# Hybrid trunk kernel, first part rebuilt: a convolution tile on TensorE, softmax order, shared copies, new weight slots

## Chip, cores and metric

One Trainium2 chip, one core. The metric is the device time of one execution in microseconds (us); of several executions the median is given. All data are 32-bit floats.

## What is computed

Two layers over 256 tokens of width 1024. In each layer a vector `c` gives six modulation vectors (shift, scale, gate for each half). The first half is attention over selected keys beside a convolution module, the second a product-key expert lookup:

```python
mod = (silu(c) @ w_ada[l] + b_ada[l])                 # 1024 x 6144 weights a layer
sh1, sc1, g1, sh2, sc2, g2 = split(mod, 6)
h = rms_norm(x) * (1 + sc1) + sh1
q, k, v, qi, ki, wi, cu = split(h @ w_in[l], offs)
attn = dsa_attention(q, k, v, qi, ki, wi)             # top 64 keys by an index score, 8 heads
a, g = split(cu, 2); u = a * sigmoid(g)
conv = silu(layer_norm(depthwise_conv31(u) + conv_b)) # 512 channels, 31 taps, causal
mixed = concat([rms_norm(attn), rms_norm(conv)])
x = x + g1 * (mixed @ w_out[l])
h2 = rms_norm(x) * (1 + sc2) + sh2
s = (h2 @ w_q) against sub_keys                       # 8 heads, 2 x top 16 of 128, then top 16 of the sums
x = x + g2 * sum_e softmax(top_s) * gelu(u_e . h2) * v_e   # 128 rows of peer_u and of peer_v a token
```

## The kernel before

The 256 tokens are two tiles of 128, and there are two layers, so the work is in four parts, p = 2 * layer + tile. Each part has a first half (`first`, then `attend`) and a second (`second`). For the expert lookup a part gathers 128 rows of `peer_u` and then 128 rows of `peer_v` for every token: 512 indirect DMAs of each in the whole kernel, each of one row of 4 KB for each of 128 partitions, issued by POOL (`u_item`, `v_item`). DVE takes the dot product of each gathered `u` row with h2 (`dots_to`), PE adds up the `v` rows (`v_to`). The rows land in a ring of 13 slots (`rows`); POOL waits for a slot before it issues (`wait_slot_free`), and for the chosen experts: the first 16 rows of part 0 wait for `head_ready`, the next 16 and then each block of 32 for `sel_ready`. DVE raises these after `choose` and `decode` of blocks 0 to 3, and between the blocks of part 0 it has fixed numbers of dot products to do (`FIRST_DOTS`: none, then up to 14, 30 and 46).

All other weights come through SP, in one order that a planner writes out (`plan`, list `seq`). A block of weights has two pieces (512 columns, in descriptors of 2 KB) or four (kinds in `WIDE`: 1024 columns, 4 KB), each piece 1 MB. Until the first part is over there are 13 slots for them: four in `wring`, others in memory that is used otherwise later (slots 4 to 9 are places of `rows`, 10 is `diag_eq`, 11 and 12 are `spread_c`). Later only the four of `wring` are left. SP issues the pieces strictly in the plan's order, and before each it waits until the piece that held the slot has been used (`wait_weight_used`); a piece on a slot that is not free holds back all behind it. `LATE_SLOT` (9) also waits for `conv_full`, because the convolution's sum `acc` lies there. `SLOTS_OF` places the later blocks of the first part by hand.

The modulation vectors of both layers are computed piecewise in between. `("ada", l, j)` is a product by PE (four pieces), `("adaT", l, j)` its turn into columns or its spreading to rows; the dictionary `ADA` says at which place of the program (`"conv"`, `"S"`, `"mix"`, `"out"`, `"wq0"`, ...) each one stands, and plan, PE and ACT follow it alike. Two of them (0, 2) and (0, 4) are computed by DVE (`ada_product`, blocks `adav`).

The jobs of PE pass through a ring of four PSUM banks (0 to 3) in the order of `seq`; ACT or DVE takes each out and frees the bank. PE, ACT and DVE each run their part of the program in a fixed order.

Part 0 in the order of PE: products (0, 0) and (0, 1), turn of h (`turn_h`) and of the modulation, `proj_turned_wide` for the convolution's input, then qi, ki, q, the index scores, k, v, products (1, 0) and (1, 1) (place `"conv"`), turns of q and k, logits, turned probabilities, the turn of the convolution's sums (waits for DVE and POOL), `values`, the turns of the sub-keys, place `"mix"`, the turn of `mixed` (`mT`), the output projection, place `"out"`, the turn of h2, and then the expert queries: `proj_heads` (two jobs of block `wq` 0), `proj_turned` (blocks 1 to 3), with subkeys and the places `"wq0"` to `"wq3"` in between. Then comes `project(1)`, which is the input projection of part 1. The convolution of part 0 runs as 31 multiply-adds for each of four channel tiles of 128: tiles 0 to 2 on DVE (`taps`, in four portions between other work, `TAP_STEPS`), tile 3 on POOL. In parts 1 to 3 it runs on PE with diagonal matrices made by ACT (L902). DVE's `glu(1)` is between its blocks 2 and 3 and waits for `ca` and `cg` of `project(1)`.

Of the kernel before, what the change touches and what calls it, by code (L numbers as in the profile page):

```python
# [16 lines left out]
P = 128  # L17
# [48 lines left out]
TAP_STEPS = (24, 18, 25)  # L66
# [6 lines left out]
def turn(l, j):  # L73
# [59 lines left out]
def plan():  # L133
# [30 lines left out]
    for p in range(PARTS):  # L164
# [15 lines left out]
        if p == 0:  # L180
# [9 lines left out]
            for name in ("k", "v"):  # L190
                both(name, p)
# [21 lines left out]
        if p == 0:  # L213
            for i in range(2):
                job("lnB", l, i)
            ada(p, "S")
# [4 lines left out]
        if p == 0:  # L221
            both("sk", p)
            ada(p, "mix")
# [4 lines left out]
        else:  # L228
# [3 lines left out]
            ada(p, "out")  # L232
        for q in range(2):
            job("h2T", p, q)
# [26 lines left out]
def trunk(nc, x, c, positions, w_ada, b_ada, w_in, q_norm_g, k_norm_g, idx_k_ln_g, idx_k_ln_b,  # L261
# [53 lines left out]
    with ExitStack() as ctx:  # L315
# [127 lines left out]
        conv_dve = sem("conv_dve")  # L443
        conv_pool = sem("conv_pool")
# [70 lines left out]
        def wait_weight_used(eng, i):  # L515

            name = uses[i][0]
            if uses[i] in vec_count:
# [37 lines left out]
        def tap_diag(p, n, j):  # L556

            return diags[:, n % 2, j, :]

# [27 lines left out]
        def _(sp):  # L587
            sp.dma_start(ccol[:, :], c[0, :].rearrange("(p k) -> p k", k=KT)).then_inc(c_landed, 16)

            def source(name, h):  # L590
# [9 lines left out]
                if kind in WIDE:  # L600
                    a = 1024 * name[2] if a is None else a
                    return w[:, 2 * h:2 * h + 2, a:a + 1024]
                a = 512 * name[2] if a is None else a
# [3 lines left out]
            for i, (name, h) in enumerate(uses):  # L607
# [25 lines left out]
                else:  # L633
                    w = weight_slot(slot).rearrange("p (k n) -> p k n", k=2 if name[0] in WIDE else 4)
# [68 lines left out]
        def _(pe):  # L703
# [120 lines left out]
            def proj_heads(block, rhs, between):  # L824

                w = [piece(block, 0), piece(block, 1)]
                for c, name in enumerate(jobs_of(block)):
                    if c:
                        between()
                    b, o = open_job(*name)  # L830
                    for i in range(2):
                        for k in range(KT):
                            at = (2 * c + i) * P
                            ins = pe.matmul(o[:, i * P:(i + 1) * P], w[k // 4][:, k % 4, at:at + P], rhs[:, k, :],
# [167 lines left out]

            def first(p):
# [25 lines left out]
                def subkey_turns():  # L1029
# [942 lines left out]
```

## Time and profile before

| | us |
|---|---|
| median of 3 runs | 1902.33 |
| lowest and highest | 1896.08, 1903.36 |
| span of the profiled execution | 1733.4 |
| own time of the profiled execution, with what lies around the span | 1902.3 (the median; 168.9 around the span) |
| bytes moved | 691.98 MB, mean 399 GB/s |

The profile is of one execution. Its span is from the first to the last instruction; what lies around it is taken as the difference of span and median, since the profiled execution has no other time. The 16 DMA engines are busy almost throughout: 9 tenths or more in nearly every slice of the page. PE is busy for 60% of the span, DVE 64%, POOL 59%, ACT 16%.

### The profile page before, as it was taken

What the parts mean: (1) busy time and instruction counts of PE and PEld (TensorE: products, weight loads), DVE (VectorE), ACT (ScalarE), POOL (GpSimd) and SP (SyncE); (2) the same over time, 40 slices, a digit from 0 to 9 for tenths busy, and PEclk for the clock granted to TensorE, in tenths of its full rate; (3) what the DMA queues carried; (4) which work ended last, traced back from release to release, by engine and by line L of the source; (5) the groups of instructions that cost most, each with busy time, mean ns of one, the idle gap of its engine ahead of it and who ended that gap; (6) DMA issues with size and microseconds to landing.
All of it is one profiled execution on the core that took longest, in us unless ns stands there. A gap on an engine that the chain in (4) does not pass through costs nothing.

```text
span 1733.4 us, 18207 instructions
## 1 busy us (share of the span) xinstructions
PE 1039.2 (60%) x6158; PEld 590.6 (34%) x6158; DVE 1103.2 (64%) x3003; ACT 273.4 (16%) x717; POOL 1015.9 (59%) x1133
## 2 busy tenths in 40 slices
PE   7979897406896588603788569611689610005555
PEld 4547674303363156301345146500236200001111
DVE  1987989996218576888117676889513979991000
ACT  2141235202110035300101024400210100000000
POOL 2610435676655763566755664567655777776774
PEclk8989899657998799655899679765899865557888
DMA  9998999999999999999999999999999999999998
GB/s 373 393 368 327 405 405 383 409 409 409 409 409 407 408 404 410 397 410 397 410 409 409 394 409 408 399 407 409 406 406 402 391 410 410 409 410 389 409 409 330
DMA packets 195481, 691.98 MB, mean 399 GB/s; under 512 B 21360, under 2 KB 21376, under 8 KB 195134
## 3 DMA queue, kind: packets, MB, share of 16 engines
q0 software_dynamic: 147840, 537.06, 78.1%
q1 hardware_dynamic: 47550, 153.77, 22.8%
q8 instruction: 49, 0.80, 0.2%
q14 instruction: 42, 0.34, 0.1%
HBM read 689.71 MB, written 1.05 MB: 398 GB/s over the span
## 4 chain that ended last, share of the span: by engine, by line
DMA 41%; PE 24%; DVE 15%; POOL 13%; issue 6%; ACT 1%; SPq 0%; DVEq 0%; ACTq 0%; POOLq 0%
DMA rows<-in_peer_v,v_at 20%; DMA rows<-in_peer_u,u_at 18%; PE ps L921 8%; DVE rows L1586 8%; PE ps L876 7%; POOL rows L698 7%; POOL rows L690 6%; DMA kiw<-in_w_in 1%; PE ps L818 1%; PE ps L864 1%; PE ps L848 1%; DMA rows<-in_w_ada 1%; DVE rows L1568 1%; PE ps L735 1%; PE ps L804 1%
## 5 line engine op out<-in xcount | busy, mean ns | idle before, releaser
L690 POOL DMA_INDIRECT rows<-in_peer_u,u_at x512 | 482.5, 942 | 370.8 <-DVE dots L1586 202.5
L1586 DVE CUSTOM_DVE_ANT_0 rows<-rows,ps 128x1024 f32<-128x1024 f32 x512 | 610.3, 1219 | 92.5 <-DMA rows<-in_peer_u,u_at 78.6
L698 POOL DMA_INDIRECT rows<-in_peer_v,v_at x512 | 485.7, 949 | 283.9 <-PE ps L921 153.4
L921 PE MATMUL ps<-rows,spread_c 128*32 128x512 f32 x2048 | 325.7, 764 | 215.0 <-DMA rows<-in_peer_v,v_at 215.0
L735 PE MATMUL ps<-ident 128*128 128x128 f32 x228 | 39.9, 346 | 354.3 <-DVE dots L1586 354.3
L921 PEld LDWEIGHTS ps<-rows,spread_c 128*32 128x32 f32 x2048 | 71.4, 125 | 414.8 <-issue 412.6
L735 PEld LDWEIGHTS ps<-ident 128*128 128x128 f32 x228 | 35.6, 183 | 369.8 <-DVE dots L1586 356.6
L876 PEld LDWEIGHTS ps<-hT,wring 128*128 128x128 f32 x1152 | 137.0, 199 | 25.7 <-issue 24.1
L876 PE MATMUL ps<-hT,wring 128*128 128x128 f32 x1152 | 142.2, 285 | 0.0
L848 PE MATMUL ps<-wring,hT 128*128 128x512 f32 x256 | 117.1, 600 | 8.3 <-DMA wring<-in_w_in 7.5
L902 PE MATMUL ps<-diag_eq,hc 128*128 128x128 f32 x744 | 104.7, 307 | 25.3 <-ACT diag_eq L1274 25.2
L1274 ACT ACTIVATE diag_eq<-ident,cwT 128x128 f32<-128x128 f32 x372 | 111.6, 387 | 30.4 <-PE ps L902 29.1
L902 PEld LDWEIGHTS ps<-diag_eq,hc 128*128 128x128 f32 x744 | 100.7, 220 | 31.6 <-ACT diag_eq L1274 29.8
L1599 DVE TENSOR_TENSOR gy<-ps,g 128x512 f32<-128x512 f32 x8 | 5.5, 689 | 162.3 <-PE ps L921 162.2
L1796 DVE MAX8 v<-mixed_use 128x8 f32<-128x128 f32 x64 | 15.7, 286 | 122.0 <-ACTq L1234 120.1
L1231 ACT COPY mixed_use<-ps 128x512 f32<-128x512 f32 (+1 forms) x54 | 30.7, 569 | 294.1 <-PE ps L876 157.9
L848 PEld LDWEIGHTS ps<-wring,hT 128*128 128x128 f32 x256 | 46.1, 190 | 69.5 <-issue 53.5
L1495 ACT ACTIVATE dots<-dots 128x128 f32<-128x128 f32 x4 | 1.2, 309 | 381.8 <-DVE dots L1586 381.8
L1895 DVE TENSOR_TENSOR gy<-ps,g 128x512 f32<-128x512 f32 x8 | 5.5, 692 | 73.1 <-PE ps L848 70.4
L1586 DVE DVE_READ_ACCUMULATOR2_ANT dots<- 128x1 f32 x512 | 42.1, 82 | 0.0
L1242 ACT ACTIVATE hT<-ps,modcol 128x128 f32<-128x128 f32 x52 | 19.5, 456 | 135.0 <-PE ps L729 134.3
L788 PE MATMUL ps<-wring,cact 128*32 128x512 f32 x192 | 27.1, 683 | 7.0 <-DMA wring<-in_w_ada 7.0
(254 smaller groups left out, 1183.9 us busy)
## 6 DMA issues: line engine op xcount, KB each, us to landing
wring<-in_w_in SPq DMA_DIRECT2D x34, 1024.0 KB, 13.2
wring<-in_w_ada SPq DMA_DIRECT2D x31, 1024.0 KB, 10.6
wring<-in_peer_wq SPq DMA_DIRECT2D x28, 1024.0 KB, 9.6
rows<-in_w_ada SPq DMA_DIRECT2D x16, 1024.0 KB, 14.9
wring<-in_w_out SPq DMA_DIRECT2D x13, 1024.0 KB, 17.1
rows<-in_peer_u,u_at POOLq DMA_INDIRECT x512, 14.1
rows<-in_peer_v,v_at POOLq DMA_INDIRECT x512, 9.5
rows<-in_w_in SPq DMA_DIRECT2D x6, 1024.0 KB, 15.9
```

Source lines behind the costliest of these rows:

```text
L690: pool.indirect_dma_start(row(n), None, u_rows, bass.IndirectOffsetOnAxis(ap=u_at[:, p % 2, k:k + 1], axis=0)).then_inc(row_landed[n % SLO ...
L698: pool.indirect_dma_start(row(n), None, v_rows, bass.IndirectOffsetOnAxis(ap=v_at[:, p % 2, tok:tok + 1], axis=0)).then_inc(row_landed[n % ...
L735: pe.transpose(ps[:, spare, 0:P], ident[:, :], ident[:, :])
L788: ins = pe.matmul(o[32 * g:32 * g + 32, :], cact[:, k:k + 1].to_broadcast([P, 32]), ws[:, i, 512 * cc:512 * cc + 512], start=h == 0, stop= ...
L848: ins = pe.matmul(o, lhs[:, k, :], w[:, j, 512 * cc:512 * cc + 512], start=k == 0, stop=k == KT - 1)
L876: ins = pe.matmul(o[:, i * P:(i + 1) * P], w[:, j, at:at + P], rhs[:, k, :], start=False, stop=(k, i) == (KT - 1, 3))
L902: ins = pe.matmul(o[:, cols], hc[:, ct, t * P + i:t * P + i + P], tap_diag(p, n, i - i0), start=False, stop=i == TAPS - 1)
L921: ins = pe.matmul(ps[32 * g:32 * g + 32, YB + q, :], spread_c[:, g, a, :], row(n)[:, q * 512:q * 512 + 512], start=a == 0, stop=a == 31)
L1231: act.copy(dst, o if src is None else src(o)).then_inc(free[b], 1)
L1242: ins = act.activation(hT[:, k, :], o[:, i * P:(i + 1) * P], ACT.Identity, bias=0.0 if shift is None else shift[:, k:k + 1], scale=scale[: ...
L1274: ins = act.activation(tap_diag(p, n, i - i0), ident[:, :], ACT.Copy, scale=cwT[:, ct, i:i + 1])
L1586: dve.tensor_tensor_reduce(out=row(n), in0=row(n), in1=h2_shown, scale=1.0, scalar=0.0, op0=ALU.mult, op1=ALU.add, accum_out=dots[:, k:k + ...
```

## The change

In part 0:

- Channel tile 0 of the convolution moves from DVE to PE (`conv_first`, 31 matmuls and one for the bias, after k). ACT makes its 31 diagonal matrices ahead in `g1`, `g2` and `skT` (`first_diag`). DVE has 62 steps in place of 93, all before the logits.
- v's projection and `lnB` change places on PE: `lnB` after k, v after the logits. The convolution's sums are turned right after v, ahead of the softmax's turned probabilities, without the 20 spare transposes; three tiles are turned, not four. ACT loads its exponential's table ahead.
- Of h's eight copies from PSUM ACT makes four and DVE four; the turn of (0, 0) comes ahead of the product (0, 1).
- The places of the modulation blocks are new: product (0, 3) and turn (0, 2) at `"conv"`, turn (0, 3) at `"S"`, product (1, 0) at `"mix"`, product (1, 1) at `"wq0"`, turn (1, 0) and product (1, 3) at `"wq1"`, turn (1, 1) and product (1, 4) at the new `"wq2"`. The sub-keys are loaded and turned after the output projection.
- `SLOTS_OF` is new. Block `wq` 0 is loaded as two pieces by head, 256 columns each (descriptors of 1 KB), so its first piece is free after the first head's job.

```diff
-TAP_STEPS = (24, 18, 25)
+TAP_STEPS = (24, 18, 20)
...
-    (0, "pre2"): [product(0, 1)],
-    (0, "preT"): [turn(0, 0), turn(0, 1)],
-    (0, "conv"): [product(1, 0), product(1, 1)],
-    (0, "S"): [turn(1, 0), turn(1, 1)],
-    (0, "mix"): [turn(0, 2), product(0, 3)],
-    (0, "out"): [turn(0, 3), turn(0, 4)],
-    (0, "wq0"): [product(1, 3)],
-    (0, "wq1"): [product(1, 4)],
+    (0, "pre2"): [turn(0, 0), product(0, 1)],
+    (0, "preT"): [turn(0, 1)],
+    (0, "conv"): [product(0, 3), turn(0, 2)],
+    (0, "S"): [turn(0, 3)],
+    (0, "mix"): [product(1, 0)],
+    (0, "out"): [turn(0, 4)],
+    (0, "wq0"): [product(1, 1)],
+    (0, "wq1"): [turn(1, 0), product(1, 3)],
+    (0, "wq2"): [turn(1, 1), product(1, 4)],
...
-SLOTS_OF = {("sk", 0): (2,), ("ada", 0, 3): (3, 4, 5, 6), ("out", 0, 0): (7, 8), ("adav", 0, 4): (0, 1, LATE_SLOT, 2),
-            ("out", 0, 1): (DIAG_SLOT, 3), ("wq", 0, 0): (5, 6), ("ada", 1, 3): (4, 7, 0, 8), ("wq", 0, 1): (1, LATE_SLOT),
-            ("ada", 1, 4): (2, DIAG_SLOT, 3, 5), ("wq", 0, 2): (0, 6), ("wq", 0, 3): (1, 2)}
+SLOTS_OF = {("ada", 0, 3): (4, 5, 6, 7), ("out", 0, 0): (8, 3), ("ada", 1, 0): (DIAG_SLOT, 0, 1, 2),
+            ("adav", 0, 4): (4, 5, 6, 7), ("out", 0, 1): (LATE_SLOT, DIAG_SLOT), ("sk", 0): (0,), ("wq", 0, 0): (1, 2),
+            ("ada", 1, 1): (4, 8, 5, 3), ("wq", 0, 1): (6, DIAG_SLOT), ("ada", 1, 3): (0, 1, 4, 5), ("wq", 0, 2): (3, 2),
+            ("ada", 1, 4): (DIAG_SLOT, 0, 1, 3), ("wq", 0, 3): (2, DIAG_SLOT)}
...
@@ wait_weight_used
-            if uses[i] in vec_count:
+            if uses[i] == (("wq", 0, 0), 0):
+                b, n = bank(("qp", 0, 0, 0))
+                eng.wait_ge(full[b], n)
+            elif uses[i] in vec_count:
...
+            def conv_first():
+
+                o = ps[:, CONV_BANK, 0:P]
+                pe.wait_ge(consts_made, 1)
+                pe.wait_ge(glu_done, 1)
+                pe.matmul(o, ident[0:TAPS + 1, TAPS:TAPS + 1].to_broadcast([TAPS + 1, P]), cw_raw[0:TAPS + 1, 0:P],
+                          start=True, stop=False)
+                for i in range(TAPS):
+                    if i % 8 == 0:
+                        pe.wait_ge(first_diag_ready, i // 8 + 1)
+                    pe.matmul(o, hc[:, 0, i:i + P], first_diag(i), start=False, stop=i == TAPS - 1)
...
@@ PE, first
                     proj(("k", p), hT)
-                    proj(("v", p), hT)
+                    spread_ln(l)
+                    conv_first()
                     ada(p, "conv")
...
                     for n in ns[:2]:
                         logits(p, n)
-                    spread_ln(l)
+                    proj(("v", p), hT)
+                    pe.wait_ge(conv_dve, CT - 2)
+                    pe.wait_ge(conv_pool, 1)
+                    for ct in range(1, CT):
+                        ins = pe.transpose(ps[:, CONV_BANK, ct * P:(ct + 1) * P], acc[:, ct, :], ident[:, :])
+                    ins.then_inc(conv_full, 1)
                     ada(p, "S")
-                    pe.wait_ge(proj_ready, 5)
                     for n in ns:
                         pe.wait_ge(exp_ready, n + 1)
                         turn4(("PT", l, n), [ex[:, n % 2, j * P:(j + 1) * P] for j in range(4)])
-                    stay_busy(20)
-                    pe.wait_ge(conv_dve, CT - 1)
-                    pe.wait_ge(conv_pool, 1)
-                    for ct in range(CT):
-                        ins = pe.transpose(ps[:, CONV_BANK, ct * P:(ct + 1) * P], acc[:, ct, :], ident[:, :])
-                    ins.then_inc(conv_full, 1)
+                    pe.wait_ge(proj_ready, 5)
                     for n in ns:
                         values(p, n)
-                    subkey_turns()
                     ada(p, "mix")
...
@@ PE, second
                 if p == 0:
-                    stay_busy(10)
+                    subkey_turns(p)
+                    stay_busy(4)
                 pe.wait_ge(h2_ready, p + 1)
...
@@ ACT, second
                     act.sem_inc(mod_ready, 1)
+                    copy_subkeys(p)
...
@@ DVE
-            tap_steps = [(i, ct) for i in range(TAPS) for ct in range(CT - 1)]
+            tap_steps = [(i, ct) for i in range(TAPS) for ct in range(1, CT - 1)]
```

## Rows read from the trace of the kernel before

**Rows 1.** Page: GB/s in 40 equal slices, two lines of costliest groups.

```profile
GB/s 373 393 368 327 405 405 383 409 409 409 409 409 407 408 404 410 397 410 397 410 409 409 394 409 408 399 407 409 406 406 402 391 410 410 409 410 389 409 409 330
...
L902 PE MATMUL ps<-diag_eq,hc 128*128 128x128 f32 x744 | 104.7, 307 | 25.3 <-ACT diag_eq L1274 25.2
...
L1274 ACT ACTIVATE diag_eq<-ident,cwT 128x128 f32<-128x128 f32 x372 | 111.6, 387 | 30.4 <-PE ps L902 29.1
```

**Rows 2.** Windows (us, busy by engine, PEclk, DMA share, GB/s), two stretches.

```profile
110.00:120.00 10.00, 10.00 (x62) 8.78 (x60) 4.50 (x13) 3.20 (x4) 0.00 (x0) 0.79 0.83 307
...
160.00:170.00 10.00, 9.49 (x86) 8.82 (x79) 8.89 (x49) 1.33 (x3) 1.45 (x2) 1.00 0.45 157
```

**Rows 3.** Chain that ended last, 186 to 232 us: start, us, what.

```profile
188.55 5.45 issue
...
194.00 10.04 PE ps L818 x64
...
211.85 16.82 PE ps L876 x128
...
229.39 0.70 DVE hc L1656
```

**Rows 4.** Timeline of POOL: start, us, instruction, [idle before <-releaser].

```profile
168.24 1.10 POOL L690 DMA_INDIRECT rows<-in_peer_u,u_at  x1 [72.13 <-DVE u_at L1864]
...
231.76 0.94 POOL L690 DMA_INDIRECT rows<-in_peer_u,u_at  x1 [20.58 <-DVE dots L1586]
...
264.93 0.94 POOL L690 DMA_INDIRECT rows<-in_peer_u,u_at  x1 [13.61 <-DVE dots L1586]
```

**Rows 5.** DMA queues, 180 to 184 us: packets, MB, share.

```profile
q0 software_dynamic: 286, 1.04, 66.0%
q1 hardware_dynamic: 285, 0.56, 36.9%
```

**Rows 6.** DMA queues, 196 to 200 us, another kind of block.

```profile
q1 hardware_dynamic: 210, 0.84, 52.9%
q0 software_dynamic: 213, 0.76, 47.8%
```

**Rows 7.** DMA issues, 164 to 168 us: size, us to landing.

```profile
rows<-in_w_ada SPq DMA_DIRECT2D x1, 1024.0 KB, 5.7
...
rows<-in_peer_wq SPq DMA_DIRECT2D x1, 1024.0 KB, 13.9
```

**Rows 8.** Timeline of PE: start, us, instruction, count, [idle before <-releaser].

```profile
30.14 1.03 PE L774 MATMUL ps<-halves,stages 128*128 128x2 f32 x8
...
84.86 3.64 PE L788 MATMUL ps<-wring,cact 128*32 128x512 f32 x32
...
94.19 1.09 PE L729 MATMUL ps<-ident,pj 128*128 128x128 f32 x8
...
118.36 1.12 PE L752 MATMUL ps<-brow,ident 24*128 24x512 f32 x2
...
126.63 1.09 PE L729 MATMUL ps<-ident,hb 128*128 128x128 f32 x8 [0.42 <-DVE hb L1791]
...
129.07 7.13 PE L804 MATMUL ps<-rows,hT 128*128 128x512 f32 x16 [1.35 <-DVEq L1888]
...
151.93 3.74 PE L834 MATMUL ps<-hT,rows 128*128 128x128 f32 x32
...
171.63 1.06 PE L818 MATMUL ps<-hT,rows 128*128 128x128 f32 x8
```

**Rows 9.** Timeline of DVE.

```profile
102.62 6.13 DVE L1568 SCALAR_TENSOR_TENSOR rows<-hc,cwT,rows 128x128 f32<-128x128 f32 x23
...
115.08 0.70 DVE L1778 BATCH_NORM_STATS2 bn<-ps 128x6 f32<-128x512 f32 x1 [5.09 <-PE ps L1095]
```

**Rows 10.** Timeline of ACT.

```profile
117.16 4.48 ACT L1231 COPY skT<-ps 128x512 f32<-128x512 f32 x4 [6.14 <-PE ps L729]
```

**Rows 11.** Windows, after a long idle of PE.

```profile
194.00:199.00 5.00, 5.00 (x23) 5.00 (x24) 5.00 (x9) 0.00 (x0) 3.63 (x4) 0.50 1.03 407
```

More of the change, by code:

```diff
@@ L189, in plan @@
                 job("dot", l, n)
-            for name in ("k", "v"):
-                both(name, p)
+            both("k", p)
+            for i in range(2):
+                job("lnB", l, i)
             ada(p, "conv")
@@ L213, in plan @@
         if p == 0:
-            for i in range(2):
-                job("lnB", l, i)
+            both("v", p)
             ada(p, "S")
@@ L232, in plan @@
             ada(p, "out")
+            both("sk", p)
         for q in range(2):
@@ L824, in proj_heads @@
             def proj_heads(block, rhs, between):
-                w = [piece(block, 0), piece(block, 1)]
                 for c, name in enumerate(jobs_of(block)):
@@ L829, in proj_heads @@
                         between()
+                    w = piece(block, c, KT)
                     b, o = open_job(*name)
@@ L1001, in project, with subkey_turns @@
                 conv(p, 5)
+            def subkey_turns(p):
+                raw = piece(("sk", p), 0, 16)
+                for n in range(4):
+                    turn4(("skT", p, n), [raw[:, 4 * n + i, :] for i in range(4)])
+            def conv_first():
[8 more added lines that the diff above has]
+                    pe.matmul(o, hc[:, 0, i:i + P], first_diag(i), start=False, stop=i == TAPS - 1)
             def first(p):
@@ L1028, in first @@
                 ada(p, "preT")
-                def subkey_turns():
-                    raw = piece(("sk", p), 0, 16)
-                    for n in range(4):
-                        turn4(("skT", p, n), [raw[:, 4 * n + i, :] for i in range(4)])
                 def index_dots():
@@ L1280, in copy_h @@
                 if p == 0:
[L1281 to L1284 removed]
+                    act.wait_ge(h0_full, 1)
+                    for k in range(4):
+                        ins = act.activation(hT[:, k, :], ps[:, HB, k * P:(k + 1) * P], ACT.Identity,
                                              bias=modcol[:, l, 0, k:k + 1], scale=modcol[:, l, 1, k:k + 1])
[L1286 to L1287 removed]
+                    ins.then_inc(hT_ready, 1)
                     return
@@ L1372, in first @@
                 if p == 0:
+                    for i in range(TAPS):
+                        ins = act.activation(first_diag(i), ident[:, :], ACT.Copy, scale=cwT[:, 0, i:i + 1])
+                        if i % 8 == 7 or i == TAPS - 1:
+                            ins.then_inc(first_diag_ready, 1)
                     sigmoid(p)
@@ L1427, in attend @@
                 if p == 0:
-                    copy_ln(l)
+                    seq_(act.activation(rsum[:, 0:1], ident[:, 0:1], ACT.Exp))
+                    for n in ns:
+                        exponentials(n)
+                    evac(("v", p), vals[:, t, :], proj_ready)
                     ada(p, "S")
                     for n in ns:
-                        exponentials(n)
-                    for n in ns:
                         turned_out(n)
-                    copy_subkeys(p)
                 else:
@@ L1716, in first @@
                 elif p == 0:
+                    dve.wait_ge(h0_full, 2)
+                    dve.wait_ge(first_mod_ready, 1)
+                    for i in range(4):
+                        k = 4 + i
+                        ins = ts(hT[:, k, :], ps[:, HB + 1, i * P:(i + 1) * P], modcol[:, l, 1, k:k + 1],
+                                 modcol[:, l, 0, k:k + 1], ALU.mult, ALU.add)
+                    ins.then_inc(hT_ready, 1)
                     dve.wait_ge(cact_made, 1)
@@ L1947, in _ @@
             take_y(PARTS - 1)
-STAGE_PLACES = [(p, where) for p in range(PARTS) for where in ("pre", "pre2", "preT", "conv", "S", "mix", "out", "wq0", "wq1", "wq3", "tail")]
+STAGE_PLACES = [(p, where) for p in range(PARTS) for where in ("pre", "pre2", "preT", "conv", "S", "mix", "out", "wq0", "wq1", "wq2", "wq3", "tail")]
 _INS = ["x", "c", "positions", "w_ada", "b_ada", "w_in", "q_norm_g", "k_norm_g", "idx_k_ln_g",
```

32 lines of the change are left out of this document (16 added, 16 removed).

## The prediction

> **What bounds the kernel now.** The page comes first [rows 1]. Most slices stand at 409 or 410: the DMA engines are the limit, and the time is bytes over that rate plus the time in which they have nothing to do. The change moves the same bytes, so it can only win or lose idle DMA time. Slices 1 to 4 (0 to 173 us) show 373, 393, 368 and 327. Against 410 they lack 43.3 x (37 + 17 + 42 + 83) / 410 = 19 us, some 4 of it at the start. The windows find the rest [rows 2]: 110 to 120 us ran at 307 GB/s (2.5 us lost), 160 to 170 at 157 (6.2 us lost). There SP waits for slots and POOL has no expert yet.
>
> It is tempting to say that part 0's end comes earlier and all of it is gained. So the chain is read next [rows 3], from where the gathers have begun: PE waits 5.45 us for nothing that the profile shows (a landing weight piece; the next job is block `wq` 3, whose two pieces it needs), starts at 194.00, takes 10.04 us, and after the turns `project(1)` follows at 211.85 for 16.8 us. Only then, at 229.39, DVE gets its `glu(1)`. DVE stands between two portions of dot products there, so rows stop too: POOL issues one at 231.76 after 20.58 us of idling [rows 4]. 16 dot products and block 3's choice later, rows start again at 264.93 [rows 4]: that is 264.93 - 229.39 = 35.5 us behind `glu(1)`. Around there the DMA engines ran dry (slice 7 at 383 GB/s, 2.9 us lost). A queue that has run dry keeps no head start. **So the time of `glu(1)`, not the first gather, sets when the rest begins**, and everything behind is again bytes over rate.
>
> What decides when PE can go on there is how fast weight pieces land beside gathers. From 180 to 184 us the gather queue q0 sent 286 packets and the weight queue q1 285 [rows 5]: one for one. A row's packet is 4 KB and one of `wq` 2 KB, so weights got 0.56 MB in 4 us, and a piece (1.05 MB) takes 7.4 us. With pieces of 4 KB descriptors q1 had 0.84 MB in 4 us [rows 6], so 5.0 us a piece. On idle engines a piece landed 5.7 us from its issue, and one queued a moment later, when rows had begun, 13.9 us [rows 7].
>
> **The change, first part.** Terms are against the profiled execution (span 1733.4, with what lies around it 1902.3, which is the median).
>
> *Before the softmax.* The turn of (0, 0) ahead of its product and four of h's copies on DVE let `cacg` start about 1.1 us earlier, the length of that turn ([rows 8], row of 30.14). On PE, v (7.1, [rows 8], row of 129.07) and products (1, 0), (1, 1) leave the stretch: products 3.6 each (row of 84.86), and 84.86 + 7.2 to the turn at 94.19 leaves 2.1 of waits for landing pieces. Together 16.4. In come product (0, 3) (3.6), turn (0, 2) (four matmuls of 1.1, row of 118.36: 4.5), `lnB` (two of that width, at most 2.2; I take 1.6) and `conv_first`. This has 32 matmuls, priced by 104.7 / 372 = 0.28 from [rows 1]: 9.0 us; the nearest row of the first part, 3.74 for 16 at full clock ([rows 8], 151.93), would make it 7.5. I take 8.0. Sum 17.7. With the 1.1 gained the turn of q and k stays at about 94.2 (bounds -0.8 to +1.3). ACT's 31 diagonals (0.387 each [rows 1], 12 us) lie under `cacg`, which takes PE 16; without that cover they would cost 12.
>
> *Logits to `mixed`.* DVE's last 26 steps (6.13 for 23, [rows 9]) are gone, and the sums are turned once v is through: logits end near 98.4, v at 105.5, three turns 0.8, so DVE starts its norm at 106.5 where it was 115.08 and had waited 5.09 [rows 9]. That is -8.6. Turned probabilities and `values` now lie under the norm. Behind DVE's norm everything follows as before: `mT` at 118.0 for 126.63 [rows 8].
>
> *A new hole on PE.* Product (1, 0) ends near 114 and `mT` comes at 118, without the 20 spare transposes. The trace shows what such an idle does: after 5.45 us the clock of the next 5 us was 0.50, that is 1.2 GHz [rows 11]. The projection would take up to 2.5 us more, or nothing if the clock holds; I take 1.2. The Trainium skill (TensorE: Matmul & The Clock Gate, HAM oscillation) has the rule that a group of matmuls behind a long wait starts at half rate again; by it alone the term would be the full 2.5, and the sum 1.3 us more.
>
> *To the queries.* The sub-keys' copies, 4.48 us on ACT [rows 10], now stand between the modulation and h2's copies. They begin when PE's output projection and turn (0, 4) are over, and end some 7 us behind the projection, about when h2's turns come out: 0 to 1.5 us. Turn (0, 3), as long as (0, 0)'s 1.0, has gone from there. I set these off. Queries start at 151.93 - 8.6 + 1.2 = **144.5**, 7.4 us earlier, and the first gather at 168.24 - 7.4 = 160.8.
>
> **The change, weights.** What is still to be loaded when gathers start? SP stalls on slots in the new table: out (0, 1)'s second piece waits for product (1, 0), product (1, 3)'s second for the first query job. I follow the order: DMA is dry for some 3 us around 110, and 5 to 6 us from 142 to 148. At the first gather's issue 53 or 54 pieces have landed, before it was 56. So even up to there the engines have gained only about 1 us.
>
> Then: product (1, 4)'s first piece sits in slot 10, which block `wq` 1's second piece holds. PE finished that block at 172.7 ([rows 8], 171.63 + 1.06), 20.8 us behind the start of the queries; the work between is the same size, so now 165.3. SP is held until then, while rows run. Behind it come six pieces that block `wq` 3 needs: four of product (1, 4) and two of `wq` 3. Before, product (1, 4)'s had all been issued by 164.4, ahead of the rows. Now: first piece 6 us, three more at 5.0 [rows 6], two at 7.4 [rows 5]: 35.8. Last one lands at **201.1**, PE starts at 201.1 where it was 194.00 [rows 3]: +7.1. PE is again cold there, as before, so 10.04 and all up to `glu(1)` moves with it: 236.5. DVE comes there earlier and waits some 20 us. The rows' restart moves from 264.93 to 272, and since the engines have run dry, the end moves as well. Sum: +7.1 on span and time: 1740.5 and **1909.4**.
>
> Product (1, 1), turns (1, 0), (1, 1) add 5.4 us of PE work behind the queries; they lie within this landing wait, and would cost at most 5.4 without it.
>
> Bounds: start of queries 141 to 148 moves the end one for one (-3.5 to +3.5); weights at 5.0 and 7.4 us if rows are always waiting, at 2.6 if they never are. The latter would have PE set the pace, and the end would come by the engines' own gain (below).
>
> **Rivals.** Half a per cent, 9.5 us, is about what a measurement of this kernel can tell from no change.
>
> *B, the head start is kept.* Rows are short while weights load (rows 6 to 11 wait for product (1, 3) and `wq` 1), so the pieces land by 190 and `glu(1)` comes before 229. For it: POOL idled in [rows 4] for slots too. Against: six rows are issued in the first 7.5 us and take twice that to transfer. Then the gain is at most the engines' own 1 us and the 2.9 at the end of the choices, perhaps 1 or 2 from `stay_busy`: -5, 1897. Chance 0.22.
>
> *C, the whole start moves.* The holes I count at 110 and 142 don't occur, because pieces are freed earlier than I follow, and the 8.7 us of [rows 2] vanish beside the 2.9: about -11, 1891. For it: 7.4 us shorter compute. Chance 0.13.
>
> *D, slower.* The mechanism of the forecast from a later start: the hole on PE keeps TensorE at 1.2 GHz through both projections (14 us at full clock, up to +5), which carries the SP stall on slot 10 along; queries at 148 to 149, last piece at 205. +11 to +12, 1914. It decides from a start of the queries at 147. Chance 0.25.
>
> **How the numbers follow.** The forecast, +1 to +9.5 with +7 as its middle, has 0.40. Faster by over 0.5%: C alone, 0.13. Slower by over 0.5%: D, 0.25. Within: forecast and B, 0.62. The range leaves out most of C and the far end of D: 1893 to 1917. The forecast's own range is 1903 to 1912.
>
> **What would show it.** After's profile should have `mT` at 118, the queries' first job (proj_heads) near 144.5, the first gather near 161; PE idle for over 10 us before block `wq` 3, which starts near 201; `glu(1)` at 236; DVE's wait for it near 20 us; rows' restart at 272; rate under 409 in the slices at 210 to 270. If PE's wait before block `wq` 3 is short and `glu(1)` comes before 229, the landing argument is wrong; if the first gather comes later than 164, the first part is.

## The result, and the profile after

The changed kernel takes 1916.28 us (median of 10 executions, 1905.60 to 1923.93), the kernel before 1903.44 in as many on the same chip (1896.08 to 1913.61): ratio 1.0062, 95% interval 1.0038 to 1.0086. It is slower, clear of noise; the interval takes in the bound of 0.5% that the prediction drew. The forecast was 1909.4, +7.1; measured are +12.8 by the medians, +11.8 by the ratio. That lies inside the range of 1893 to 1917, near its end, and above the forecast's own range of 1903 to 1912.

One thing ahead of all comparisons. The profiled execution of after has a span of 1905.7 and an own time of 1907.86: 2.2 us lie around the span, not the 168.9 that the prediction took. The kernel before was therefore profiled again ("before, second profile": time 1896.14, span 1894.3). The execution behind [rows 1 to 11], with its 1733.4, was an unusually fast one: none of the other executions timed of this kernel was under 1881. The page of after, and under it the same line of the second profile of before:

```profile
GB/s 376 393 337 303 353 309 348 382 410 288 359 409 407 380 361 384 263 394 356 358 392 408 406 350 356 301 378 410 319 377 409 392 362 381 369 380 310 369 366 318
...
L1301 ACT ACTIVATE diag_eq<-ident,cwT 128x128 f32<-128x128 f32 x372 | 111.7, 387 | 127.3 <-remote 87.1
```

```profile
L1274 ACT ACTIVATE diag_eq<-ident,cwT 128x128 f32<-128x128 f32 x372 | 111.7, 387 | 138.4 <-remote 84.2
```

[Rows 1] have 409 or 410 in most slices and 30.4 us of idle time before these copies, put down to PE. Here most slices are lower and the idle time is 127 to 138 us, mostly put down to "remote": the release came when no work of this core had just ended. So a typical execution loses some 160 us to something that the first profile does not have. An idle time by "remote" holds the ordinary wait for PE as well. The stall proper is what passes from the end of PE's work to the release, and it is given so below.

The stages of part 0, in us:

| | first profile | second profile | forecast | after |
|---|---|---|---|---|
| turn of the convolution's sums | 114.34 | 115.72 | 105.7 | 107.34 |
| `mT` on PE | 126.63 | 128.00 | 118.0 | 119.51 |
| first query job | 151.93 | 153.20 | 144.5 | 147.01 |
| first gather | 168.24 | 169.6 | 160.8 | 163.4 |
| block `wq` 3 starts | 194.00 | 195.30 | 201.1 | 217.49 |
| `glu(1)` | 229.39 | 244.44 | 236.5 | 252.16 |
| rows' restart (44th row) | 264.93 | 283.2 | 272 | 291.1 |
| 128th row (last of `peer_u`, part 0) | 381.7 | 411.7 | | 419.6 |
| last row's issue | 1718.0 | 1882.5 | | 1893.8 |

Against the second profile the queries come 6.2 us earlier (forecast 7.4), and the rows' restart 7.9 later (forecast 7.1). The last row is 11.3 later. A difference between two single executions is no finer than their scatter: the second profile's time is 6.5 us above the median of the kernel before on its chip (1889.60), that of after is 8.4 below its median, and the two were not timed in turns.

PE of after around the new hole (timeline: start, us, instruction, idle before):

```profile
119.51 1.97 PE L745 MATMUL ps<-ident,hb 128*128 128x128 f32 x8 [3.76 <-DVE hb L1827]
122.82 5.26 PE L820 MATMUL ps<-rows,hT 128*128 128x512 f32 x8 [1.35 <-DVEq L1924]
127.92 3.60 PE L820 MATMUL ps<-wring,hT 128*128 128x512 f32 x8
...
147.01 3.84 PE L849 MATMUL ps<-hT,wring 128*128 128x128 f32 x32 [1.27 <-ACTq L1273]
...
172.85 2.08 PE L1197 MATMUL ps<-skT,mixed_use 128*128 128x128 f32 x8 [4.98 <-ACTq L1261]
```

The idle of 3.76 us costs 1.97 for a turn of 1.09 ([rows 8], 126.63) and 5.26 for a projection piece of 3.60: 2.5 us. The granted clock (windows: us, busy by engine, PEclk, DMA share, GB/s) fell to 0.50, which is 1.2 GHz, and then came back:

```profile
119.50:124.50 5.00, 3.64 (x10) 2.41 (x11) 2.73 (x6) 1.14 (x4) 0.00 (x0) 0.50 1.06 351
124.50:130.00 5.50, 5.50 (x12) 2.38 (x11) 5.36 (x5) 0.00 (x0) 0.00 (x0) 0.86 0.98 305
```

The sub-keys' copies hold the first query job back by 1.27.

The chain that ended last, of after, from block `wq` 2 on:

```profile
191.72 2.54 PE ps L834 x11
...
194.27 13.69 DMA wring<-in_peer_wq
207.96 9.53 issue
217.49 9.35 PE ps L834 x64
```

SP's queue of after in the same stretch:

```profile
172.16 0.37 SPq L652 DMA_DIRECT2D diag_eq<-in_w_ada  x1
178.78 14.15 SPq L652 DMA_DIRECT2D wring<-in_w_ada  x3
194.27 0.37 SPq L652 DMA_DIRECT2D wring<-in_peer_wq  x1
204.40 0.37 SPq L652 DMA_DIRECT2D diag_eq<-in_peer_wq  x1
```

The pieces are issued late, and mostly not because of pieces queued ahead. Four things can be read off:

- The first piece of product (1, 4) is issued at 172.16, where 165.3 was forecast. PE had ended block `wq` 1 at 167.88; ACT's release by the same block came at 172.17. So 4.3 us of that are a stall, which holds SP as well as ACT.
- The last piece of product (1, 4) takes slot 3. Block `wq` 2's first piece holds it until about 192.5, and so the piece goes out at 192.56 only. From 188 to 194 the weight queue q1 sent nothing, and rows had the engines to themselves (DMA queues: packets, MB, share; q0 is the only one):

```profile
q0 software_dynamic: 685, 2.51, 102.2%
```

- Piece 0 of `wq` 3 takes slot 2, which `wq` 2's second piece holds until 194.27, where PE ends that block. It lands 13.7 us later, at 207.96.
- Piece 1 takes slot 10 (`diag_eq`), which the first piece of product (1, 4) holds until PE has used it near 200.8. It is issued at 204.40, another 3.6 us later, and PE starts 13.1 us behind that. As piece 0 was still landing then, this late issue cost little: 9.4 us pass between the two landings, where 7.4 was forecast.

The DMA queues from 204 to 218 us:

```profile
q0 software_dynamic: 1008, 3.68, 66.7%
q1 hardware_dynamic: 887, 1.99, 36.8%
...
diag_eq<-in_peer_wq SPq DMA_DIRECT2D x1, 1024.0 KB, 13.0
```

Rows and weights share the engines nearly packet for packet, as in [rows 5]. By the Trainium skill (DMA: Bandwidth & Descriptors, Queues, rings and completion order) an engine takes turns between the queue rows that have work for it; the counts agree.

The same stretch of the chain in the second profile of before:

```profile
191.67 0.59 ACT mixed_use L1231
...
192.30 23.05 another core or an unknown queue
...
215.37 0.59 ACT mixed_use L1231
...
258.12 11.24 another core or an unknown queue
```

Before block `wq` 3 PE waited 3.67 us there and ended it at 205, but ACT did not take it out of PSUM before 215.37: a stall of 10.4 us. It does not stand in [rows 3], where the block's end and `project(1)` are 7.8 us apart. It hid part of what the change adds. After has a stall of 7.1 us there too (ACT released at 212.49, PE's product (1, 4) over at 205.3), but it ends inside the wait for `wq` 3 and costs nothing.

### The profile page after: what moved, and what is told of

It reads as the page before. It is cut to its first block, busy times and chain, and to the rows that moved or that the text cites. A ratio compares the mean times of both kernels' runs of the same rounds, so it can differ in the third digit from the quotient of the medians.

```text
span 1905.7 us, 18286 instructions
## 1 busy us (share of the span) xinstructions
PE 1113.3 (58%) x6195; PEld 630.3 (33%) x6195; DVE 1087.4 (57%) x2976; ACT 281.2 (15%) x745; POOL 1017.1 (53%) x1133
## 4 chain that ended last, share of the span: by engine, by line
PE 29%; another core or an unknown queue 20%; issue 14%; DMA 12%; DVE 11%; POOL 7%; ACT 5%; SPq 0%; ACTq 0%; DVEq 0%; POOLq 0%
DMA rows<-in_peer_v,v_at 8%; POOL rows L714 6%; DVE rows L1617 6%; PE ps L863 5%; PE ps L936 5%; PE ps L891 5%; PE ps L917 3%; PE ps L820 3%; ACT diag_eq L1301 2%; DMA rows<-in_w_ada 1%; DMA rows<-in_peer_u,u_at 1%; POOL rows L706 1%; PE ps L879 1%; DMA rows<-in_w_in 1%
## 5 line engine op out<-in xcount | busy, mean ns | idle before, releaser
L1617 DVE CUSTOM_DVE_ANT_0 rows<-rows,ps 128x1024 f32<-128x1024 f32 x512 | 597.2, 1218 | 60.9 <-issue 53.3
L936 PE MATMUL ps<-rows,spread_c 128*32 128x512 f32 x2048 | 333.9, 767 | 175.7 <-DMA rows<-in_peer_v,v_at 137.4
L891 PE MATMUL ps<-hT,wring 128*128 128x128 f32 x1152 | 147.5, 289 | 30.7 <-issue 30.7
L917 PE MATMUL ps<-diag_eq,hc 128*128 128x128 f32 x744 | 119.5, 329 | 74.9 <-issue 48.0
L751 PE MATMUL ps<-ident 128*128 128x128 f32 x202 | 35.1, 341 | 180.2 <-DVE dots L1617 179.1
L917 PEld LDWEIGHTS ps<-diag_eq,hc 128*128 128x128 f32 x744 | 112.9, 240 | 81.6 <-issue 49.1
L863 PE MATMUL ps<-wring,hT 128*128 128x512 f32 x256 | 123.9, 630 | 14.1 <-issue 7.1
L751 PEld LDWEIGHTS ps<-ident 128*128 128x128 f32 x202 | 30.5, 179 | 194.7 <-DVE dots L1617 180.2
L768 PE MATMUL ps<-brow,ident 24*128 24x512 f32 x16 | 12.8, 888 | 86.3 <-issue 85.5
L804 PE MATMUL ps<-wring,cact 128*32 128x512 f32 x200 | 38.6, 811 | 38.8 <-issue 19.5
```

The lines of the kernel that those rows point to most:

```text
L751: pe.transpose(ps[:, spare, 0:P], ident[:, :], ident[:, :])
L804: ins = pe.matmul(o[32 * g:32 * g + 32, :], cact[:, k:k + 1].to_broadcast([P, 32]), ws[:, i, 512 * cc:512 * cc + 512], start=h == 0, stop= ...
L863: ins = pe.matmul(o, lhs[:, k, :], w[:, j, 512 * cc:512 * cc + 512], start=k == 0, stop=k == KT - 1)
L891: ins = pe.matmul(o[:, i * P:(i + 1) * P], w[:, j, at:at + P], rhs[:, k, :], start=False, stop=(k, i) == (KT - 1, 3))
L917: ins = pe.matmul(o[:, cols], hc[:, ct, t * P + i:t * P + i + P], tap_diag(p, n, i - i0), start=False, stop=i == TAPS - 1)
L936: ins = pe.matmul(ps[32 * g:32 * g + 32, YB + q, :], spread_c[:, g, a, :], row(n)[:, q * 512:q * 512 + 512], start=a == 0, stop=a == 31)
```

## The experiments

Ratios are to the kernel before, timed in turns with it on the same chip. Its median was 1889 to 1907 us by chip and session, so the times themselves compare only through the ratios. Rows are numbered from 0 here, so the 44th is row 43.

**The kernel before once more.** No edit.

> The kernel before, unchanged, for a second profile. The profile that the prediction rests on had a span of 1733.4 us beside a median of 1902.33, that of the changed kernel a span of 1905.7 beside 1907.86. If the first was an execution with faster memory, this one has a span of about 1900 us, DMA rates near 350 to 370 GB/s in the stretches of rows as after has (363 on average), and glu(1) later than 229, at 235 to 245. If the change itself slowed the DMA engines, it shows 1733 and 409 GB/s again.

1896.14 us, span 1894.3. The 169 us between the first span and the median were not time around the execution.

**Product (1, 4) at the tail, in both kernels.** The four pieces that load beside rows, with their turn, go behind part 0's rows.

```diff
@@ after
-    (0, "wq2"): [turn(1, 1), product(1, 4)],
-    (0, "wq3"): [turn(1, 3), turn(1, 4)],
-    (0, "tail"): [product(0, 5), turn(0, 5)],
+    (0, "wq2"): [turn(1, 1)],
+    (0, "wq3"): [turn(1, 3)],
+    (0, "tail"): [product(0, 5), turn(0, 5), product(1, 4), turn(1, 4)],
...
-            ("ada", 1, 4): (DIAG_SLOT, 0, 1, 3), ("wq", 0, 3): (2, DIAG_SLOT)}
+            ("wq", 0, 3): (DIAG_SLOT, 0)}
@@ before
-    (0, "wq1"): [product(1, 4)],
...
+            ("wq", 0, 2): (2, DIAG_SLOT), ("wq", 0, 3): (3, 0)}
```

> The changed kernel with product (1, 4) and its turn moved from wq2/wq3 to the tail, behind project(1); block wq 3 takes slots 10 and 0. Nothing is left out. Landing theory (block wq 3 waits for six pieces that share the DMA engines with rows, four of them product (1, 4)'s): wq 3 starts near 195 where it was 217.5, glu(1) near 228 for 252, and the time falls by 10 to 20 us from 1916, to about 1901. Rival (the engines' bytes alone set the time, the first part's idle time is what counts): the same bytes, so 1912 to 1920.

1895.31 us, 1.0024 (0.9998 to 1.0050). Block `wq` 3 started at 199.84 in place of 217.49, `glu(1)` came at 243.44 in place of 252.16, the rows' restart at 282.2, as in the kernel before. By the ratio 0.38% (7 us) is won back where 10 to 20 us were expected; the intervals of after and of this run overlap a little. So the blocks around `wq` 3 probably carry most of the loss.

> The kernel before with product (1, 4) and its turn moved to the tail in the same way; wq 2 takes slots 2 and 10, wq 3 slots 3 and 0. Nothing is left out. Landing theory: both pieces of wq 3 are issued before or with the first rows, PE does not wait for them, glu(1) comes 12 to 20 us earlier than in the kernel before, time 1885 to 1895 for 1903. Rival (bytes alone): 1900 to 1906.

1889.65 us, 1.0012 (0.9988 to 1.0035). The rival held: the time did not fall. `glu(1)` came at 231.06 and the rows' restart at 269.8, 13.4 us earlier than in the second profile of before. By row 127 the lead was 5.7 us. Between these two profiles 7.6 us are left at the last row, but the second profile of before is itself 6.5 above its median; by the medians nothing is left. The four pieces had to be loaded later, and PE waited 10.6 us for them at the tail.

**Rows held back.** In after, POOL's first gather waits until product (1, 4) is through.

```diff
+                        wait_full(pool, ("ada", 1, 4))
```

> The changed kernel, with POOL's first gather held until product (1, 4) is done on PE, so its four pieces land without rows beside them. Nothing is left out. Landing theory: these pieces land at 2.6 to 4 us each and not at 5 or more, wq 3 starts near 197 where it was 217.5, although the first row is issued 20 us later (about 184 for 163); time 1905 to 1912, not slower than the changed kernel. Rival (the first gather sets the time): 20 us later rows cost up to 20 us, 1925 to 1935.

1901.45 us, 1.0085 (1.0057 to 1.0113). With no rows beside it, block `wq` 3 started at 194.53 in place of 217.49, though rows did not begin before 191.1: the pieces that load beside rows make the wait. SP issued the last piece at 187.58, and it took 6.9 us in place of 13.0. But the time missed what was expected (at most 1912 for 1903.44, a ratio of 1.0045), and it gained nothing on after. What can be seen in its place is that ACT then stood still (timeline of ACT):

```profile
190.22 0.58 ACT L1259 COPY stages<-ps 128x512 f32<-128x512 f32 x1 [3.50 <-PE ps L805]
229.13 0.58 ACT L1259 COPY mixed_use<-ps 128x512 f32<-128x512 f32 x1 [38.33 <-remote]
```

PE had ended block `wq` 3 at 203.4, so 25.7 of the 38.33 us are the stall. There is none ahead of the first row, and this one right behind it.

**The two halves.** From the kernel before, first the compute half alone (convolution tile, v's turn, h's copies; tables as before), then the tables alone (`ADA`, `SLOTS_OF`, sub-keys, `wq` 0 by head).

```diff
@@ compute half: as in the change, without ADA, SLOTS_OF, the sub-keys' place and wq 0
-TAP_STEPS = (24, 18, 25)
+TAP_STEPS = (24, 18, 20)
...
+                    spread_ln(l)
+                    conv_first()
@@ tables: these alone
-            ("ada", 1, 4): (2, DIAG_SLOT, 3, 5), ("wq", 0, 2): (0, 6), ("wq", 0, 3): (1, 2)}
+            ("ada", 1, 4): (DIAG_SLOT, 0, 1, 3), ("wq", 0, 3): (2, DIAG_SLOT)}
```

> Only the compute half of the change on the kernel before: convolution tile 0 on TensorE, its turn ahead of the softmax, v behind the logits, h's copies shared, exponential's table ahead. ADA, SLOTS_OF, the sub-keys' place and block wq 0 are as before. Nothing is left out. Landing theory: queries start 5 to 9 us earlier, product (1, 4) is still issued ahead of the rows, the rows' restart (44th row) comes 3 to 7 us earlier than in the kernel before, ratio to it 0.996 to 0.998. Rival (the compute half itself costs, through the idle hole on PE and the clock): ratio 1.003 or more.

1901.80 us, 0.9974 (0.9951 to 0.9998). The ratio is the expected one, the way to it is not: the convolution's sums are turned 11 us earlier (104.72), yet the queries come no earlier (154.03), and the rows' restart is not earlier either (284.6). Where the 0.26% come from is not shown, and the interval nearly touches 1. PE's time went to its clock (windows: us, busy by engine, PEclk, DMA share, GB/s):

```profile
108.00:130.00 22.00, 20.96 (x83) 10.15 (x81) 8.52 (x27) 9.75 (x15) 0.00 (x0) 0.61 0.87 330
```

The granted clock was 0.61 over 22 us, so for most of it 1.2 GHz. The sub-keys' turns took 3.62 us for 1.92, turn (0, 2) 8.0 for 4.2 in the second profile of before. In the kernel before, the 20 spare transposes stand ahead of this stretch; that they keep the clock up was not tried by itself.

> Only the other half on the kernel before: new ADA and SLOTS_OF, the sub-keys behind the output projection, block wq 0 by head, turn (0, 0) ahead of product (0, 1). The convolution, v, lnB and h's copies are as before. Nothing is left out. Landing theory: product (1, 4) and wq 3 share the engines with rows, block wq 3 starts 15 to 25 us later than in the kernel before, the 44th row 10 to 16 us later, ratio 1.006 to 1.010, more than the whole change. Rival: 1.000 to 1.003.

1924.87 us, 1.0110 (1.0081 to 1.0140). PE waited 16.61 us before block `wq` 3 (226.09, 31 us later than in the kernel before) and DVE 33.55 for `glu(1)` (261.88); the rows' restart came at 300.7, 17.5 us late. All are somewhat more than expected. The two halves add up within their intervals: -0.26% and +1.10% are +0.84%, measured together +0.62% (0.38 to 0.86).

**Product (1, 4) inside `project(1)`, behind v.** In the kernel before and in after, so that its pieces are loaded neither ahead of `glu(1)` nor at the tail.

```diff
+    (0, "mid"): [product(1, 4), turn(1, 4)],
...
             job("v", p)
+            ada(0, "mid")
```

> As the kernel before with product (1, 4) and its turn taken from wq1 and wq3, but placed in project(1) behind v, not in the tail; slots as in the tail variant. Nothing is left out. With product (1, 4) in the tail, rows restarted 13 us earlier than in the kernel before and yet the time was the same (ratio 1.0012); I think because its 4 MB (10 us) were then loaded behind the restart, in place of the dry time before it. If so, here they are loaded while the engines are dry: the 44th row at 270 to 275 and the lead kept to the end, ratio 0.994 to 0.997. Rival (the restart of the rows does not matter at all): ratio 0.999 to 1.002.

1907.13 us, 1.0007 (0.9977 to 1.0036): the rival held. Again 14 us of lead at the rows' restart (269.0), and again gone, by row 80 (349.1; second profile of before 347.0). ACT stalled in front of its diagonals, and q and k of part 1 came late to DVE:

```profile
297.35 3.03 ACT L1276 ACTIVATE diag_eq<-ident,cwT 128x128 f32<-128x128 f32 x10 [20.87 <-remote]
```

```profile
324.87 1.22 DVE L1685 TENSOR_TENSOR hb<-pj 128x1024 f32<-128x1024 f32 x1 [20.49 <-ACTq L1236]
```

> The changed kernel with product (1, 4) and its turn in project(1) behind v. Nothing is left out. By the same theory: block wq 3 starts near 196, glu(1) near 243 as with the tail (1.0024), and the 10 us of loading lie in dry time: ratio to the kernel before 0.996 to 1.000, that is 6 to 12 us faster than the changed kernel. Rival: 1.002 to 1.006.

1918.66 us, 1.0076 (1.0043 to 1.0109), above what the theory said and at the rival's upper end. Block `wq` 3 came at 198.40, `glu(1)` at 241.09, the restart 11.6 us earlier than in after; by row 80 it was 3.6 us behind after (358.6 to 355.0).

**Fewer rows in flight.** In the second profile of before and in after, every stall of ACT by "remote" lies behind the first gather. Now POOL waits, before gather n, for the landing of gather n - 4, in before and in after.

```diff
                     n = u_item(p, k)
+                    if n >= 4:
+                        wait_row(pool, n - 4)
                     wait_slot_free(pool, n)
```

> The kernel before, and POOL issues gather n only when gather n - 4 has landed, so that at most 4 rows of 128 x 4 KB are queued at the DMA engines in place of 13. Nothing else changes. Theory A (the 11 to 38 us in which ACT, and with it PE and DVE, stand still in every typical execution while rows are in flight come from the backlog of queued rows: 13 rows of 0.52 MB at 410 GB/s are 16.6 us, 4 rows 5.1 us): ACT's 23.11 us stall before 215.37 and the 11.3 us one before 269.39 shrink to 5 us or less, glu(1) comes before 232 in place of 244.44, and the time falls far below 1894, towards the 1733 of the execution that had no such stalls: 1750 to 1850. Theory B (the stalls have another cause): they stay at 11 us or more and the time stays within 1880 to 1940, the upper end if 4 rows are too few to keep the DMA engines busy beside PE's and DVE's waits.

1968.29 us, 1.0320 (1.0293 to 1.0346). The page:

```profile
GB/s 376 392 358 333 394 382 355 337 332 334 360 383 340 356 400 335 368 334 326 377 355 363 329 397 373 367 334 337 353 368 330 339 338 330 343 341 339 336 340 290
...
L692 POOL DMA_INDIRECT rows<-in_peer_u,u_at x512 | 485.3, 948 | 502.0 <-DMA rows<-in_peer_u,u_at 327.5
...
L1278 ACT ACTIVATE diag_eq<-ident,cwT 128x128 f32<-128x128 f32 x372 | 111.5, 387 | 27.3 <-PE ps L906 18.5
```

The mechanism came out as Theory A has it: the diagonals' idle time is 27.3 us, as in [rows 1], in place of 138.4, `glu(1)` came at 231.45 and the restart at 268.6. The time did not, and lies above both ranges: 4 rows are too few, the engines move some 340 GB/s in many slices, and POOL waits 327.5 us for landings.

> The changed kernel with the same limit of 4 rows in flight. Theory A: as for the kernel before, ACT's stall of 11.04 us at 172.17 goes to 5 us or less and the time falls to between 1760 and 1860; against the kernel before with the same limit it stays some 7 us slower if the landing of six weight pieces beside rows is the whole cost of the change, and equal to it within 4 us if half of the cost came from the stalls. Theory B: 1890 to 1950. By either, block wq 3 starts earlier than 217.49, since fewer queued rows share the engines with the weight pieces: near 201 as predicted at first if the stalls were what was missing.

1983.44 us, 1.0380 (1.0340 to 1.0419), 0.8% over the row above. The time missed both theories. Almost without stalls (in part 0 one of 2.2 us, inside 8.96 us of idling up to 169.19; two of about 2 us later) the changed kernel starts block `wq` 3 at 212.45, and `glu(1)` and restart come 16 and 15 us later than in the kernel before with the same limit. So 201 was wrong here too, and not through stalls. SP's queue and the chain:

```profile
175.79 11.39 SPq L652 DMA_DIRECT2D wring<-in_w_ada  x3
187.70 0.37 SPq L652 DMA_DIRECT2D wring<-in_peer_wq  x1
192.50 0.37 SPq L652 DMA_DIRECT2D diag_eq<-in_peer_wq  x1
```

```profile
187.70 17.13 DMA wring<-in_peer_wq
204.83 7.62 issue
212.45 2.69 PE ps L838 x11
```

Product (1, 4)'s last piece waits for slot 3 again and goes out near 187. PE gets it at 197.54, piece 0 of `wq` 3 lands 7.3 us behind it (204.83) and PE can start 7.6 us behind that. These are the 7.4 us a piece of the forecast. What is late is the queue's feed, held by the slots.

**Six rows in flight**, in the kernel before; the same edit with 6.

> The kernel before with at most 6 rows queued (gather n waits for the landing of gather n - 6). With 4 rows the stalls of ACT put down to no engine of the core were gone (0 us in place of 531.7 over the span), but the DMA engines moved 340 GB/s in most slices where the kernel before at its best moves 409: 4 rows of 0.524 MB at 340 GB/s say that a gather takes 6.2 us from its issue to its landing, so 410 GB/s need 4.8 rows in flight. Theory A (backlog): 6 rows are 7.7 us of transfer, 1.5 us more than the 6.2, so the engines stay full and hardly anything queues: slices back at 400 to 410, stalls of ACT under 100 us, time 1740 to 1800. Theory B (a threshold elsewhere, such as any full queue at all): with the engines full the stalls are back at over 300 us and the time is 1870 to 1910. In between, 1800 to 1870, both are partly true: stalls grow with the backlog but begin as soon as the engines are full.

1870.27 us, 0.9898 (0.9839 to 0.9957): faster than the kernel before, and by the ratios than after. The stalls are back, and shorter in sum. PE's convolution in the second profile of before (13 rows), then with 6 rows, single matmuls between which PE waits for nothing that the profile shows:

```profile
299.45 0.37 PE L902 MATMUL ps<-diag_eq,hc 128*128 128x128 f32 x1 [1.13 <-issue]
301.54 0.37 PE L902 MATMUL ps<-diag_eq,hc 128*128 128x128 f32 x1 [1.72 <-issue]
303.64 0.37 PE L902 MATMUL ps<-diag_eq,hc 128*128 128x128 f32 x1 [1.73 <-issue]
```

```profile
289.09 0.37 PE L906 MATMUL ps<-diag_eq,hc 128*128 128x128 f32 x1 [1.72 <-issue]
290.49 0.37 PE L906 MATMUL ps<-diag_eq,hc 128*128 128x128 f32 x1 [1.02 <-issue]
291.90 0.37 PE L906 MATMUL ps<-diag_eq,hc 128*128 128x128 f32 x1 [1.04 <-issue]
```

They come every 2.1 us with 13 rows and every 1.4 us with 6. That alone would prove little: in after, with up to 13 rows, some come every 1.4 us as well (188.87, 190.30, 191.72 in block `wq` 2). ACT's stall at its first diagonals of part 1 is 7.7 us (of 11.31 idle) with 13 rows and 2.6 (of 6.23) with 6. Summed over the span, from the end of the awaited work to ACT's release, the stalls put down to "remote" are roughly 220 us in the second profile of before, 150 with 6 rows and none with 4. This is an estimate, as matmul records can be missing. The 531.7 and 430 us of the expectations are the idle times; 199.5 of the 531.7 are one wait before `dots`, of which all but 5.2 is the ordinary one for DVE.

The time lies at the lower edge of Theory B. The stalls fit it: they are there as soon as the engines are nearly full, and fewer queued rows make them less. No run separates the two causes further.

**Compute half with five rows in flight.**

> The compute half of the change alone (e4: 0.9974 of before) with at most 5 rows queued. 5 rows of 0.524 MB in the 6.2 us that a gather takes are 423 GB/s, just over the 409 that the engines move at best. Theory A (stalls come from what queues beyond the engines' need): ACT's stalls put down to no engine of the core stay under 150 us (0 at 4 rows, 430 at 6), slices near 400, time 1740 to 1830. Theory B (the stalls begin as soon as the engines are full, and fewer rows only make each shorter: 11.3 us at 13 rows, 6.2 at 6): either the engines are not quite full or the stalls are back, and the time lies between that of 6 rows and that of 4: 1865 to 1930, ratio 0.985 to 1.01. If the compute half keeps its own gain under a limit, this kernel is 0.26% under what the limit alone would give, too little to be read off here.

1869.10 us, 0.9881 (0.9848 to 0.9915). Theory B holds: most slices are between 350 and 410, some near 300, and the stalls sum to about 150 us, as with 6 rows. Its interval lies inside that of 6 rows, so nothing is said on which is better; both beat the two kernels.

## Why the prediction was right or wrong

- *The first part* was right in its mechanism and a little optimistic. Set against the second profile, the convolution's sums are turned 8.4 us earlier and `mT` comes 8.5 earlier, where 8.6 was said. The queries come 6.2 us earlier where 7.4 was said; the hole on PE is the term that was too small, 2.5 us for 1.2. The Trainium skill (TensorE: Matmul & The Clock Gate, HAM oscillation) has matmuls behind a long wait start at half rate; the trace of after agrees, with a granted clock of 0.50. The sub-keys' 1.27 us lie inside the bounds.
- *Weights beside rows* was right as the cause: tables alone +1.10%, rows held back 194.53 for 217.49. **The step that failed is the list of issues**: "Last one lands at 201.1" took the six pieces as queued one behind the other from 165.3 on. But only the second and the third are (issued at 178.78 and 180.49, with the first still landing). The first is issued at 172.16, of which 4.3 us are a stall. The fourth waits for slot 3 until 192.56, and q1 is empty from 188 to 194. The last two wait for slots 2 and 10, and the last piece was issued at 204.40, later than it was to land. PE's start of the block was put at 201.1 and measured 217.49, 16 us more: 6.9 at the first issue, some 6 of empty queue, the rest in longer landings. The term of 7.1 was 22.2 against the second profile (217.49 - 195.30).
- *The restart came out near 7.1 nevertheless*, and that is luck. Two errors met: the landing wait was too small by 16 us, and the stall behind block `wq` 3 in the kernel before was unknown to the prediction. What after adds before `wq` 3 (22.2 us) is taken back by 14.5 between there and `glu(1)`: 10.4 of stall, and some 4 in which PE runs at the low clock behind it (8 matmuls of 2.08 us at 216.05, where after has 1.16 at 227.54). That these offset each other is read from the two chains; with 4 rows, where the stall is gone, the change's cost at the restart is 15 us in place of 7.9, and 14.8 at the last row, which bears it out.
- *"The time of `glu(1)` sets when the rest begins"* is half true. A delay there stays: +7.9 at the restart is +7.9 at row 127, and the tables' +17.5 is +15.8. A lead does not: 13.4 and 14.2 us of lead at the restart ended as 1.0012 and 1.0007. For the second of these, the trace shows another gate: `project(1)` on PE and ACT, whose q and k DVE took at 324.87, no earlier than in the second profile of before (322.85).
- *DMA engines bound* held only for the execution of [rows 1]. In typical ones the stalls took their share too: 363 GB/s over the span of after, 399 in the first page.
- *Forecast +7.1, measured +11.8*: the restart has 7.9 of it. The rest is not steady in the two profiles (+7.9 at row 127, +4.6 at 511, +7.2 at 639, +11.3 at 767 and at the last), and no run here tells where it arises, or how much of it is the scatter of executions.
- *Rivals.* D had the right size (+11 to +12) by the wrong mechanism: its condition, queries from 147 on, was just met (147.01), but its price was a slow clock through both projections, of which one piece was slow. B and C would have needed `glu(1)` no later than before; it came at 252.16 for 244.44.

The path by which queued rows hold up ACT, PE, DVE and SP stays open. That the number of queued rows is what matters is shown in the kernel before (no stalls by "remote" at 4, less at 6 than at 13); what it is that waits behind them is not. Instruction fetches were my first suspect. The Trainium skill (Runtime: NRT & Kernel Launch, Instruction fetch mechanics) has each engine fetch its instructions in blocks of 16 KiB through a DMA queue of its own, the cost mostly hidden. The trace speaks against them as what ends a stall. The queues of the second profile of before from 262 to 269.3 us, up to the end of ACT's 11.31:

```profile
q0 software_dynamic: 511, 1.87, 63.6%
q1 hardware_dynamic: 313, 1.16, 39.2%
```

No instruction packet lands there, nor from 200 to 215.3, up to the end of the 23.11. Also open is why the first profiled execution had no stalls with the same 13 slots. One rival was not tried: the recording itself. The trace of the first execution holds 22,885 updates of semaphores, that of the second profile, of the same program, only 11,256. After has 10,917, 6 rows 12,324 and 4 rows 19,618. So where there are stalls, about half of the updates left no record. Every execution timed here has a span and a clock out of its own record, so none shows whether the kernel stalls, or gains from fewer rows in flight, when nothing is recorded.

## What to carry to other kernels

When a table of buffer slots is changed, write beside every transfer of the critical block, and of those queued ahead of it, who holds its slot and when that one is done: a piece that is issued late leaves the queue empty, and then lands beside other traffic, here in 13 us in place of 7. Profile a kernel twice and hold the span against the timed median: a gap of 9% was no overhead here but another execution. An idle time is not a stall: take off what the engine had to wait for anyway. Where gathers are queued as deep as buffers allow, try fewer in flight; six in place of 13 took 1.0% off, more than any other single edit here.

## What was not expected of the hardware

- The same program ran once with a span of 1733.4 us and otherwise near 1894, at 399 and some 363 GB/s.
- With up to 13 gathers of 0.52 MB queued, ACT was released 2.5 to 25.7 us behind the end of PE's work that it waited for (the stalls read in part 0 and at the start of part 1); with 6 its first such stall was 2.6 us, with 4 the kernel before had none.
- With 4 gathers in flight the DMA engines moved some 340 GB/s, so a gather took about 4 x 0.524 MB / 340 GB/s = 6.2 us from its issue to its landing. By that sum 410 GB/s need 4.8 in flight; with 5 most slices stood between 350 and 410.
